# Both projections of the hybrid block as seven block products per pair of chunks, and two expert loads issued earlier

## The reference

```
h = rmsnorm(x, norm1_g)
u, q, k, v, g_pool, g_attn = split(h @ w_in, [512, 512, 128, 128, 1024, 1024])
y_pool = multiscale_pool(u, pool_w, pool_scale) @ w_pool_proj      # (256, 512) @ (512, 1024)
y_attn = sliding_window_attention(q, k, v, ...) @ w_attn_proj      # (256, 512) @ (512, 1024)
mixed  = sigmoid(g_pool) * y_pool + sigmoid(g_attn) * y_attn
x = x + mixed @ w_out
x = x + moe(rmsnorm(x, norm2_g), ...)   # 32 experts, 4 per token, each 1024x2048 up and 1024x1024 down
return rmsnorm(x, final_g)
```

## Time and profile before

| | |
|---|---|
| median of three executions | 1081.47 us |
| the profiled execution | 1082.4 us |
| its span, first to last instruction | 1080.5 us |
| TensorE busy | 1017.8 us (94%) |
| VectorE / ScalarE / GpSimd busy | 267.8 / 103.2 / 63.5 us |
| HBM read | 428.17 MB, 397 GB/s over the span |
| chain that ended last | TensorE 74%, DMA 18% |
| mean granted TensorE clock | 0.984 |

### The profile page before, as it was taken

One profiled execution on the slowest core, in us unless ns is written; L12 is line 12 of the kernel. 1 busy time (PEld: TensorE's weight loads), 2 busy tenths in 40 slices (PEclk: granted clock), 3 DMA queues, 4 the chain that ended last, 5 costly groups with the idle time before them and its releaser, 6 DMA issues.

```text
span 1080.5 us, 11893 instructions
## 1 busy us (share of the span) xinstructions
PE 1017.8 (94%) x5112; PEld 483.5 (45%) x5112; DVE 267.8 (25%) x642; ACT 103.2 (10%) x227; POOL 63.5 (6%) x58
## 2 busy tenths in 40 slices
PE   9999999999999999889989898989899999999997
PEld 8999985333333333333333333333333333333332
DVE  3543333212131212121203022121212120313022
ACT  2130022101010101000000001010100000000012
POOL 1453300200000000000000000000000000000001
PEclk9999999999999999999999999999999999999999
DMA  9904998999999999999999999999999999999995
GB/s 337 352 2 169 415 389 315 420 422 428 428 436 420 436 429 431 432 429 431 432 431 428 432 436 427 428 432 437 429 428 429 437 421 429 427 426 428 425 421 215
DMA packets 37730, 430.03 MB, mean 398 GB/s; under 512 B 6139, under 2 KB 7852, under 8 KB 18092
## 3 DMA queue, kind: packets, MB, share of 16 engines
q1 hardware_dynamic: 33216, 427.04, 93.7%
q10 hardware_dynamic: 4156, 1.14, 0.5%
q0 software_dynamic: 304, 1.06, 0.3%
HBM read 428.17 MB, written 1.06 MB: 397 GB/s over the span
## 4 chain that ended last, share of the span: by engine, by line
PE 74%; DMA 18%; SPq 2%; issue 2%; ACT 1%; DVE 1%; POOL 0%; POOLq 0%; DVEq 0%
PE bank L1174 29%; PE bank L1181 19%; DMA ring<-in_w_down 15%; PE bank L944 5%; PE bank L1154 4%; PE bank L1108 4%; DMA ring<-in_w_up 3%; PE bank L1018 3%; PE bank L954 3%; SPq L440 2%; PE bank L875 2%; PE bank L1137 1%; PE bank L1147 1%; PE bank L889 1%; ACT h_buf L772 1%
## 5 line engine op out<-in xcount | busy, mean ns | idle before, releaser
L1174 PE MATMUL bank<-ring,z_buf 128*64 128x512 f32 x2032 | 457.1, 601 | 20.9 <-issue 16.6
L1174 PEld LDWEIGHTS bank<-ring,z_buf 128*64 128x64 f32 x2032 | 148.2, 138 | 313.1 <-issue 312.9
L1181 PE MATMUL bank<-ring,h_buf 128*64 128x512 f32 x960 | 220.0, 612 | 29.0 <-DMA ring<-in_w_down 17.5
L1181 PEld LDWEIGHTS bank<-ring,h_buf 128*64 128x64 f32 x960 | 71.4, 141 | 157.1 <-issue 141.4
L1692 DVE COPY y<-bank 128x256 f32<-128x256 f32 x32 | 12.1, 420 | 272.0 <-PE bank L1181 272.0
L1108 PEld LDWEIGHTS bank<-u_buf,m_buf 128*128 128x128 f32 x512 | 59.7, 192 | 22.0 <-issue 21.9
L1108 PE MATMUL bank<-u_buf,m_buf 128*128 128x128 f32 x512 | 65.4, 281 | 0.0
L1661 DVE TENSOR_TENSOR z_buf<-bank,g2x 128x512 f32<-128x512 f32 (+1 forms) x33 | 22.3, 675 | 170.0 <-PE bank L1108 169.0
L1700 DVE TENSOR_SCALAR swi<-bank 128x256 f32<-128x256 f32 x64 | 27.2, 425 | 146.4 <-PE bank L1174 141.2
L1154 PE MATMUL bank<-y,u_buf 128*128 128x512 f32 x120 | 54.1, 593 | 0.0
L656 POOL TENSOR_TENSOR m_buf<-acc,ring 128x512 f32<-128x512 f32 x2 | 2.5, 1275 | 861.4 <-DVE acc L1670 861.3
(11 more groups left out here) (217 smaller groups left out, 591.2 us busy)
## 6 DMA issues: line engine op xcount, KB each, us to landing
ring<-in_w_up SPq DMA_DIRECT2D x40, 4096.0 KB, 24.3
ring<-in_w_down SPq DMA_DIRECT2D x20, 4096.0 KB, 22.6
ring<-in_w_up SPq DMA_DIRECT2D x38, 2048.0 KB, 27.3
ring<-in_w_down SPq DMA_DIRECT2D x24, 1024.0 KB, 26.4
ring<-in_w_down SPq DMA_DIRECT2D x11, 2048.0 KB, 20.1
ring<-in_w_up SPq DMA_DIRECT2D x18, 1024.0 KB, 9.5
ring<-in_w_in SPq DMA_DIRECT2D x5, 2048.0 KB, 22.1
ring<-in_w_out SPq DMA_DIRECT2D x2, 2048.0 KB, 12.9
```

The source lines that it names most:

```text
L1174: ins = nc.tensor.matmul(up_banks[j][e * SLOTS:(e + 1) * SLOTS, :], xgT[:, k, e * SLOTS:(e + 1) * SLOTS], row[:, j * CH:(j + 1) * CH], sta ...
L1181: ins = nc.tensor.matmul(banks[n][e * SLOTS:(e + 1) * SLOTS, :], of[:, k, e * SLOTS:(e + 1) * SLOTS], w[e].rearrange("p (k n) -> p k n", k ...
```

## The change

The projections are now made like the gates. `proj_weights(j)` gives the four weight blocks of a pair; contraction halves are 2 chunks (256) each, so a product is 2 matmuls of 128 tokens. GpSimd makes four more sums per pair (`r1` to `r4`, 128x256 each, in `proj_sums`), always directly behind the gate's; VectorE makes `q1` to `q4` from `pooledT` and from `attnT` (`sum_rhs`, once for each branch; each of the four waits for the one whose result it needs). TensorE's order inside `gate_pair` interleaves the two: `x`, `px`, `z`, `pz`, then behind `sum_read` again `x`, `px`, `y_`, `py`, `v`, `pv`, then behind the second `sum_read` `y_`, `py`, `x`, `px`. `product_done` now counts 5 per pair. `read_first` and `read_second` read both parts; `read_other` does for the projection what `read_third` does for the gate, and frees the banks; `mix` works on SBUF alone, 512 columns in one instruction. On VectorE the four instructions of `sum_rhs(pooledT, 0)` stand ahead of the bias additions, `read_second(0)` has moved ahead of the last three instructions of the softmax's maxima, and `mix(2)` behind `read_first(3)`, `mix(3)` behind the sums of the attention and `read_first(4)`. On SyncE the expert loads 0 and 2 of the first pass are issued after `gate0b` and `gate2b`, ahead of the wait for `attn1`.

```diff
         hT_sums = ring[:, C_U % R, 0:2048].rearrange("p (i k t) -> p i k t", i=4, k=KD // 2)
         w_sums = ring[:, C_Q % R, 0:2048].rearrange("p (i k n) -> p i k n", i=4, k=KD // 2)
+        rhs_sums = [ring[:, C_U % R, 2048 + n * D:2048 + (n + 1) * D].rearrange("p (i k t) -> p i k t", i=4, k=KW // 2) for n in range(2)]
+        proj_sums = ring[:, C_Q % R, 3072:4096].rearrange("p (i k n) -> p i k n", i=4, k=KW // 2)
...
+        def proj_weights(j):
+            c = 2 * (j % (LAST_POOL + 1))
+            n = W_POOL if j <= LAST_POOL else W_ATTN
+            w = ring[:, n % R, :].rearrange("p (k n) -> p k n", n=D)
+            low, high = slice(0, KW // 2), slice(KW // 2, KW)
+            first, second = slice(c * P, (c + 1) * P), slice((c + 1) * P, (c + 2) * P)
+            return n, (w[:, low, first], w[:, high, first], w[:, low, second], w[:, high, second])
...
+            for load, free in ((0, "gate0b"), (2, f"gate{LAST_POOL - 1}b")):
+                sp.wait_ge(unit_done, UNIT[free] + 1)
+                load_expert(slot_of(FIRST, load), load, FIRST)
...
-            for load in (2, 3, 0, 4, 6, 5, 1, 8, 9, 10):
+            for load in (3, 4, 6, 5, 1, 8, 9, 10):
...
                 nc.gpsimd.tensor_tensor(s1, a21, a22, ALU.add).then_inc(w_sum_ready, 1)
-                pool.wait_ge(w_sum_ready, 4 * j + 1)
+                pool.wait_ge(*load_at(n_proj))
+                nc.gpsimd.tensor_tensor(r1, p21, p22, ALU.add).then_inc(w_sum_ready, 1)
+                pool.wait_ge(w_sum_ready, 8 * j + 1)
                 if j >= 1:
                     pool.wait_ge(product_done, PRODUCTS * (j - 1) + 3)
                 nc.gpsimd.tensor_tensor(s2, s1, a11, ALU.subtract).then_inc(w_sum_ready, 1)
-                pool.wait_ge(w_sum_ready, 4 * j + 2)
+                pool.wait_ge(w_sum_ready, 8 * j + 2)
+                nc.gpsimd.tensor_tensor(r2, r1, p11, ALU.subtract).then_inc(w_sum_ready, 1)
+                pool.wait_ge(w_sum_ready, 8 * j + 4)
                 if j >= 1:
                     pool.wait_ge(product_done, PRODUCTS * (j - 1) + 4)
                 nc.gpsimd.tensor_tensor(s3, a11, a21, ALU.subtract).then_inc(w_sum_ready, 1)
+                nc.gpsimd.tensor_tensor(r3, p11, p21, ALU.subtract).then_inc(w_sum_ready, 1)
...
                 nc.gpsimd.tensor_tensor(s4, a12, s2, ALU.subtract).then_inc(w_sum_ready, 1)
+                nc.gpsimd.tensor_tensor(r4, p12, r2, ALU.subtract).then_inc(w_sum_ready, 1)
...
-                product(x, a11, b11, opens=True, closes=False).then_inc(product_done, 1)
+                product(x, a11, b11, opens=True, closes=False)
+                if j in (0, LAST_POOL + 1):
+                    pe.wait_ge(*load_at(n_proj))
+                    pe.wait_ge(*emptied_at("pool1" if j == 0 else "attn1"))
+                product(px, p11, c11, opens=False, closes=False).then_inc(product_done, 1)
                 pe.wait_ge(hT_sums_ready, 4)
-                pe.wait_ge(w_sum_ready, 4 * j + 1)
-                product(z, s1, t1, opens=True).then_inc(product_done, 1)
-                product(v, a22, t4, opens=False)
+                pe.wait_ge(w_sum_ready, 8 * j + 1)
+                product(z, s1, t1, opens=True)
+                pe.wait_ge(rhs_sums_ready, 4 * (of + 1))
+                pe.wait_ge(w_sum_ready, 8 * j + 2)
+                product(pz, r1, q1, opens=False).then_inc(product_done, 1)
                 pe.wait_ge(sum_read, 2 * j + 1)
                 product(x, a12, b21, opens=False)
-                project_other(a[:, SEQ:2 * SEQ], c)
-                pe.wait_ge(w_sum_ready, 4 * j + 2)
-                product(y_, s2, t2, opens=False, closes=False).then_inc(product_done, 1)
-                project_other(b[:, SEQ:2 * SEQ], c + 1)
+                product(px, p12, c21, opens=False)
+                pe.wait_ge(w_sum_ready, 8 * j + 4)
+                product(y_, s2, t2, opens=False, closes=False)
+                product(py, r2, q2, opens=False, closes=False).then_inc(product_done, 1)
+                product(v, a22, t4, opens=False)
+                product(pv, p22, q4, opens=False)
                 pe.wait_ge(sum_read, 2 * j + 2)
-                pe.wait_ge(w_sum_ready, 4 * j + 3)
-                product(y_, s3, t3, opens=False).then_inc(product_done, 1)
-                pe.wait_ge(w_sum_ready, 4 * j + 4)
-                product(x, s4, b22, opens=True).then_inc(unit_done, 2)
+                pe.wait_ge(w_sum_ready, 8 * j + 6)
+                product(y_, s3, t3, opens=False)
+                product(py, r3, q3, opens=False).then_inc(product_done, 1)
+                pe.wait_ge(w_sum_ready, 8 * j + 8)
+                product(x, s4, b22, opens=True).then_inc(product_done, 1)
+                product(px, r4, c22, opens=True).then_inc(unit_done, 2)
...
+            def sum_rhs(rhs, of):
+                low, high = rhs[:, 0:KW // 2, :], rhs[:, KW // 2:KW, :]
+                q1, q2, q3, q4 = (rhs_sums[of][:, i] for i in range(4))
+                nc.vector.tensor_tensor(q1, low[:, :, P:SEQ], low[:, :, 0:P], ALU.subtract).then_inc(rhs_sums_ready, 1)
+                nc.vector.tensor_tensor(q3, high[:, :, P:SEQ], low[:, :, P:SEQ], ALU.subtract).then_inc(rhs_sums_ready, 1)
+                dve.wait_ge(rhs_sums_ready, 4 * of + 1)
+                nc.vector.tensor_tensor(q2, high[:, :, P:SEQ], q1, ALU.subtract).then_inc(rhs_sums_ready, 1)
+                dve.wait_ge(rhs_sums_ready, 4 * of + 3)
+                nc.vector.tensor_tensor(q4, q2, high[:, :, 0:P], ALU.subtract).then_inc(rhs_sums_ready, 1)
+            dve.wait_ge(*emptied_at("pool1"))
+            sum_rhs(pooledT, 0)
...
             def read_first(j):
-                x, y_, z, v = regions(j)
+                x, y_, px, py, z, v, pz, pv = regions(j)
+                p, o = pre[j % 2], other(j)
                 dve.wait_ge(product_done, PRODUCTS * j + 1)
                 if j >= 2:
-                    dve.wait_ge(*emptied_at(f"gate{j - 2}b"))
-                nc.vector.tensor_copy(pre[j % 2][:, 2 * P:3 * P], x).then_inc(sum_read, 1)
+                    dve.wait_ge(mix_done, j - 1)
+                nc.vector.tensor_copy(p[:, 2 * P:3 * P], x)
+                nc.vector.tensor_copy(o[:, 2 * P:3 * P], px).then_inc(sum_read, 1)
             def read_second(j):
-                x, y_, z, v = regions(j)
-                p = pre[j % 2]
+                x, y_, px, py, z, v, pz, pv = regions(j)
+                p, o = pre[j % 2], other(j)
                 dve.wait_ge(product_done, PRODUCTS * j + 3)
                 dve.wait_ge(sum_read, 2 * j + 1)
                 nc.vector.tensor_copy(p[:, 0:P], x)
-                nc.vector.tensor_tensor(p[:, P:2 * P], p[:, 2 * P:3 * P], y_, ALU.add).then_inc(sum_read, 1)
...
+                nc.vector.tensor_tensor(p[:, P:2 * P], p[:, 2 * P:3 * P], y_, ALU.add)
+                nc.vector.tensor_copy(o[:, 0:P], px)
+                nc.vector.tensor_tensor(o[:, P:2 * P], o[:, 2 * P:3 * P], py, ALU.add).then_inc(sum_read, 1)
+            def finish(p, x, y_, z, v):
...
+                return nc.vector.tensor_tensor(p[:, 3 * P:4 * P], p[:, 3 * P:4 * P], z, ALU.add)
+            def read_third(j):
+                x, y_, px, py, z, v, pz, pv = regions(j)
+                dve.wait_ge(unit_done, UNIT[f"gate{j}b"] + 1)
+                dve.wait_ge(sum_read, 2 * j + 2)
+                finish(pre[j % 2], x, y_, z, v).then_inc(pre_ready, 1)
+            def read_other(j):
+                x, y_, px, py, z, v, pz, pv = regions(j)
+                finish(other(j), px, py, pz, pv).then_inc(emptied["dve"], 2)
             def mix(j):
                 c = 2 * (j % (LAST_POOL + 1))
-                p = pre[j % 2]
+                p, o = pre[j % 2], other(j)
+                both = mixedT[:, c:c + 2, :].rearrange("p k t -> p (k t)")
                 dve.wait_ge(sig_ready, j + 1)
...
+                dve.wait_ge(*emptied_at(f"gate{j}b"))
+                if j <= LAST_POOL:
+                    nc.vector.tensor_tensor(both, o, p, ALU.mult).then_inc(mix_done, 1)
+                else:
+                    nc.vector.tensor_tensor(o, o, p, ALU.mult).then_inc(mix_done, 1)
+                    dve.wait_ge(mix_done, j + 1)
+                    nc.vector.tensor_tensor(both, both, o, ALU.add).then_inc(mixed_ready, 2)
...
             read_first(0)
             nc.vector.tensor_reduce(stat[:, 0, 0, :], scores0, AX.X, ALU.max)
             link(nc.vector.tensor_reduce(stat[:, 0, 1, :], scores1, AX.X, ALU.max))
+            read_second(0)
...
-            read_second(0)
             read_third(0)
             read_first(1)
+            read_other(0)
             dve.wait_ge(exp_ready, 1)
...
             mix(0)
             read_third(1)
             read_first(2)
+            read_other(1)
             mix(1)
             read_second(2)
             read_third(2)
-            mix(2)
+            read_other(2)
...
             read_first(LAST_POOL)
+            mix(LAST_POOL - 1)
             read_second(LAST_POOL)
```

(37 more changed lines are left out.)

33 lines of the change are left out of this document (11 added, 22 removed).

## The result

The changed kernel takes 1089.69 us (median of four, 1089.07 to 1090.74) against 1081.28 us: ratio 1.0073, 95% interval 1.0060 to 1.0086. It is 8.4 us slower; the forecast was 1084.8, 3.35 us slower, and the range ended at 1087.0. The profiled execution took 1090.74 us, its span is 1088.9 us against 1080.5.

What follows compares the result with a forecast made beforehand. The prediction took TensorE's chain in the mixer, which frees the slots for the expert-load stream, to bound the kernel. Waits of 6.0 us less 2.65 of matmuls gave +3.35 us: 1084.8 us, range 1079.6 to 1087.0.

Steps and rivals of the forecast that it cites:

- what bounds the kernel: Mixer: each microsecond TensorE takes more or less moves the first freed slot, the expert-load stream and the end equally.
- the price of a product: Gate pairs: half products of 0.89 us (gate) and 0.45 (projection); each pair without a wait 9.38 us instead of 9.71.
- the first gate: First gate: VectorE's sums, in turns with GpSimd, make the first read late; TensorE, due at 52.37, waits 4.1 us.
- Sum. Waits 4.1 + 0.35 + 1.0 + 0.25 + 0.3: Total: waits in gate 0 (two reads), gate 1, attention sums and later `mix` losses, 6.0 us; less 2.65 of matmuls, +3.35.
- the second gate's wait: Gate 1: its second read comes behind the exponentials, at R + 14.75 against R + 13.7 wanted; TensorE waits 1.0 us.
- L1559 loses a turn: Rival, VectorE ahead of gate 1's second read: GpSimd's sum goes first, 1.1 us more, 1085.9; within the forecast's 0.63.
- The second read of gate 0: First gate: VectorE's second read is done at R + 4.35, TensorE wants it at R + 4.0; wait 0.35 us.
- The attention's `sum_rhs`: Start of the attention branch: VectorE's sums of `attnT` come 0.2 to 0.5 us late for TensorE's `pz`; 0.25 taken.
- The early loads: SyncE: two loads of 4.9 us each move into an idle stretch and change nothing at the end.
- Sums that run through: Rival, first gate: VectorE's four sums end at 49.3 before GpSimd's turn; wait 1.2, total +0.4, 1081.9; chance 0.22.
- The waits off TensorE's path: Rival, mixer: VectorE's reads stand ready as early as before, only shorter projections count, -2.65, 1078.8; chance 0.10.
- The early loads shortening the stream: Rival, load queue: the dry stretch at 160 us is not one, up to 9.8 us saved, 1075.0; chance 0.05.

Runs made afterwards that it cites:

- e2: Changed kernel, but GpSimd waits for VectorE's four sums of `pooledT` before its own second sum of pair 0; 1083.93 us against 1082.12 for the kernel before.
- e7: Changed kernel with VectorE's list, and TensorE's in gates 0 and 4, reordered so nothing precedes a read TensorE is due to need; 1082.57 us against 1081.87 before.
- e9: e7 reordered again at its three waits, in the first gate of each branch and in gate 2; 1081.48 us against 1081.59 for the kernel before.
- e3: Changed kernel with extra identity matmuls on TensorE ahead of its waits in the first two gates; 1086.93 us against 1082.12 for the kernel before.
- e5: Kernel before with only VectorE's four sums of `pooledT` added ahead of the bias additions, used by nobody; 1088.06 us against 1082.12 for the kernel before.
- e4: Changed kernel with `read_second(0)` put back behind the last three instructions of the softmax's maxima; 1086.07 us against 1082.12 for the kernel before.
- e10: Changed kernel with the edits of e2 and e4 together; 1084.00 us against 1081.59 for the kernel before.
- e1: Changed kernel without the two expert loads issued early on SyncE; 1089.93 us against 1081.87 for the kernel before.
- e6: Kernel before with only the two expert loads issued early; 1081.94 us against 1081.87 for the kernel before.

## Why the prediction was wrong

**Right: what bounds the kernel.** The first half load was to leave near 178 us and left at 182.46; span and half load moved together in every run.

**Right: the price of a product.** 9.38 us per pair without a wait was forecast; gates 5, 6 and 7 of the changed kernel take 9.38, 9.41 and 9.38.

**Right, in part by luck: the first gate.** "TensorE, due at 52.37, waits 4.1 us": it waited 3.87. The sums in turns with GpSimd were laid out to end at 52.2 in a profile that starts this gate at 49.69; the new one starts it 0.5 us earlier and the sums end at 51.35. e2 shows that the turns are the cause of 2.5 us of it (1.41 stay). An unforeseen 0.5 us of issue ahead of L1559 is in the 3.87, and without it the wait would have been 3.4: two errors made up for each other. Why the 0.5 us is there in the runs in which the sums stand ahead of the additions, and not in e7 and e9, stays open.

**Wrong: "Sum. Waits 4.1 + 0.35 + 1.0 + 0.25 + 0.3".** The step that failed is that a wait was priced at its own length. Behind it TensorE's products were taken at the 1.34 us of the earlier trace rows, whose clock is 1.00. The runs showed instead that a wait of 3.87 us is followed by 5.9 us of products at half clock, 2.95 us of work lost (e3: the clock stays up when TensorE is kept at work; e5: the wait alone brings the fall). A forecast with the granted clock in it would have had 1084.8 + 2.95 = 1087.8 from the first wait alone. The Trainium skill says as much on its page "TensorE: Matmul & The Clock Gate", section "HAM oscillation — how this bites in real kernels": a TensorE that idles long enough between groups of matmuls starts the next at the lower clock. The trace agrees for the first wait; behind the second the clock fell only 1.1 us after TensorE had gone on.

The warning stood in the profile of before, outside the mixer. In the mixer its clock is 1.00 throughout, and TensorE's longest wait at the gates is 0.2 us. But in the expert passes the clock falls to 0.50 nine times, for 3.4 us each, each time at the end of or behind a wait of TensorE's of 2.1 to 3.8 us, for instance (timeline, then a stretch of TensorE):

```profile
616.07 6.50 PE L1174 MATMUL bank<-ring,z_buf 128*64 128x512 f32 x22 [2.93 <-issue]
```

```profile
616.00:618.00 2.00, 1.93 (x6) 0.50 1.14 492
```

Not every such wait draws a fall: of eleven of 2 us and more two did not, one of them 2.85 us long (it ended at 439.73). So these rows gave the fall as a likely price of a forecast wait of 4.1 us, not as a certain one.

Term by term, the two falls add 4.65 us to the forecast's 3.35, the second wait 0.99 and gate 4 0.11; the first wait is 0.23 smaller, and the 0.35 and 0.3 did not show. That makes 8.2.

**Mis-sized: the second gate's wait, 1.0 forecast, 1.99 measured.** Lost turns on VectorE added to it at two places. The rival "L1559 loses a turn" came true: that instruction (L1624 now) took 2.12 us instead of 1.2. And the three small instructions behind `read_second(0)` took 0.56, 0.65 and 0.16 us beside GpSimd, so that the exponentials started 1.27 us behind that read, not 0.5. That the exponentials stood behind the read was in the forecast; e4 shows that the wait goes without it, and e2 that it is as long (2.0 us) when the clock stays up in gate 0. The wait then drew a second fall, 1.7 us.

**The second read of gate 0, 0.35 forecast:** no wait at all, since TensorE was slow by then. There was none either in e2, whose clock was up, so 0.35 was too much by itself; with the read behind the maxima, in e10, it was 1.9 us. **The attention's `sum_rhs`:** 0.36 in gate 4, 0.25 forecast. **The early loads:** nothing, as forecast (e1, e6).

**The rivals.** Sums that run through: not so, they take turns. The waits off TensorE's path: not so in the changed kernel, and even e9 could not reach it. The early loads shortening the stream: no.

## What to carry to other kernels

When a change makes TensorE wait where it never waited, price the wait and then ask what the clock does behind it: here waits of 3.87, 3.4 and 1.99 us each came with 3.4 us or more at half speed, in which busy shares look perfect and only the clock column and the records per microsecond tell. Look for such falls in the whole profile of before, not only in the stage that the change touches: its mean clock of 0.984 was the sign. When VectorE is the late engine, look at what is put ahead of its next awaited instruction, and count GpSimd's instructions beside those whose two inputs are in SBUF; letting the engine with room wait (e2, one line) took back most of this loss. And lay out gains and losses again after each repair: slow stretches cover other waits, so repairs do not add up, and most of a saving of 0.33 us per gate on one engine was used up by waits for another that had little room.
